# First block of a two-block kernel: modulation vector in PSUM, projections by blocks, another order of stages

## The chip, the core and the metric

The kernel runs on one core of a Trainium2 chip. A core has TensorE (PE, matrix products into PSUM), VectorE (DVE), ScalarE (ACT), GpSimd (POOL), and SyncE (SP), whose queue issues all the DMAs here. Each engine takes its own instructions in order and waits on semaphores. Times are microseconds on the device; less is better. PSUM has eight banks of 512 float32 per partition; GpSimd cannot reach them.

## What is computed

Two transformer blocks over 256 tokens of width 1024. Only the first part of the first block matters here, from its inputs to its gated outputs:

```python
sh1x, sc1x, g1x, sh2x, sc2x, g2x = jnp.split((jax.nn.silu(c) @ w_ada[l] + b_ada[l])[:, None, :], N_MOD, axis=-1)
sh1c, sc1c, g1c, sh2c, sc2c, g2c = jnp.split(jax.nn.silu(c_ctx) @ w_ada[l] + b_ada[l], N_MOD, axis=-1)
hc = _modulate(_rms_norm(ctx, norm1_g[l]), sh1c, sc1c)
s_f, s_b = _context_states(hc, w_in[l], gla_w2[l], gla_b2[l], s0)
hx = _modulate(_rms_norm(x, norm1_g[l]), sh1x, sc1x)
# _token_mixer(hx, ...):
z = h @ w_in
u, vs, q, r, ga, gb, k, v, lr = _split(z, IN_SPLITS)
a = _spatial_gating(gelu(u), gelu(vs), sgu_ln_g, sgu_ln_b, sgu_w, sgu_b)
o, s_f, s_b = _gla_bidir(qh, k, v, lr, gla_w2, gla_b2, s0f, s0b)
```

`_gla_bidir` is gated linear attention in both directions: the decays come from `log_sigmoid(lr @ w2 + b2)`, their running sums give exponentials by which queries and keys are scaled, and the state of the context enters the one of the tokens. All products are made as three matmuls of float32 values split into a rounded part and a remainder (`_hi` and `_lo`).

## The kernel before

**Weights.** All large weights pass through four slots (`w_raw`, `w_hi`, `w_lo`), a unit of 1024 x 128 at a time, 512 KB. SP loads a unit into `w_raw` once `lo_ready` says that GpSimd has made the remainder of the unit that stood there; ScalarE rounds it to `w_hi` when TensorE is done with the slot (`unit_used`), and GpSimd makes `w_lo` (L567) and raises `lo_ready`. The order is w_k (units 0 to 3), w_q (4 to 7), w_v (8 to 15), w_vs (16 to 23), w_u (24 to 31), w_r and so on.

**Modulation.** The first 16 vectors of the six modulations (shift and scale before the mixer) are made on TensorE: four products of `c2` with `adab` (L882), each two rows of 512, copied to `modrow`, transposed (L889) and added to biases on VectorE. The other 32 are made on VectorE, in 16 steps of `modulations(p0, p1)`: each multiplies two rows of `w_ada` (`adaw`, 1 MB, a ring of buffers filled by `ada_rows` on SP) with `csil`, the vector silu(c) in every partition, and sums along (L2364). `row_used` counts steps.

**Split inputs.** For each pair of eight k, VectorE makes the modulated input into `hfull`, ScalarE the same rounded into `a_hi` (`modulated(j)`), and VectorE the remainder `a_lo` (L2289, `split_ready`).

**Order on TensorE.** The four products with `c2`, with the means of squares between them; `w_k` (L640, 512 columns: tokens and context), tile after tile; the low-rank projection `wlr` (L903); `w_q`; the eight logits (L914), which need VectorE's `lrs` remainder (`lr_ready`) and four banks; `w_v` by token (`lin_tokens`, L716, two units at a time, 256 columns); `scores(0)` (L933, L935), transposes of `ks` (`keys`, L949), `w_vs` in four pairs with `keys` and `states(0)` (L960, L964) between them, `scores(1)`, `keys(1)`, `w_u` with `states(1)` after its fourth tile, half of `w_r`, `spatial()` (L996), the rest of `w_r`, `outputs()`.

**VectorE and ScalarE between them.** `decays(d)` and `differences(d)` make running sums and their differences, ScalarE's `powers` and `key_powers` exponentials, `operands(d)` the scaled queries and keys for `scores(d)`. `layer_norm_stats` reads `vs`.

## Time and profile before

| | us |
|---|---|
| median of 3 runs | 1358.4 (1358.06 to 1359.99) |
| profiled execution | 1354.67 |
| its span, first to last instruction | 1352.8 |
| TensorE busy | 1306.9 (97%) |
| GpSimd busy | 880.7 (65%) |
| VectorE busy | 742.7 (55%) |
| ScalarE busy | 703.9 (52%) |
| mean granted TensorE clock | 0.982 of full |

The page of the profile gives busy shares, 40 slices of the span with the granted clock, and groups of instructions. Matmuls are pipelined, so the time of one is read from start to start and not from its duration. An "idle before" of TensorE is a wait; its releaser is inferred. The timeline merges neighbours of one kind.

### The profile page before, as it was taken

How to read it: one execution, taken by the hardware profiler on the slowest of the kernel's cores; microseconds unless marked ns; L12 is line 12 of the kernel's file. 1: busy time of each engine (PE TensorE's matmuls, PEld its weight loads, DVE VectorE, ACT ScalarE, POOL GpSimd, SP SyncE). 2: the span in 40 equal slices, each digit the busy share in tenths (PEclk: the TensorE clock that was granted, in tenths of full speed). 3: DMA queues.
4: the chain of work that ended last, by engine and by line, in shares of the span. 5: the costliest groups of instructions: out<-in, count | busy, mean ns of one | idle time of the engine just before them, and what ended most of it. 6: DMA issues, size and time to landing. Idle time of an engine off the chain costs nothing.

```text
span 1352.8 us, 28587 instructions
## 1 busy us (share of the span) xinstructions
PE 1306.9 (97%) x10351; PEld 1246.8 (92%) x10351; DVE 742.7 (55%) x1539; ACT 703.9 (52%) x1232; POOL 880.7 (65%) x367
## 2 busy tenths in 40 slices
PE   8889989999999999999999999999999999999996
PEld 3579889999989999998889999999999999999996
DVE  4899994221465565256636326655552676555632
ACT  2555435354455555458333225756665555666653
POOL 0453667478859887956223223888888787888794
PEclk9989989999999999999899899999999999999999
DMA  8864345345536555744212112555555554555562
GB/s 327 340 244 171 133 149 199 114 139 183 176 125 203 183 176 167 193 138 145 65 62 66 60 54 88 172 179 178 172 172 185 174 185 151 189 177 183 164 183 74
DMA packets 60837, 217.75 MB, mean 161 GB/s; under 512 B 9832, under 2 KB 11112, under 8 KB 57936
## 3 DMA queue, kind: packets, MB, share of 16 engines
q1 hardware_dynamic: 60752, 216.56, 49.2%
q8 instruction: 61, 1.00, 0.3%
q14 instruction: 24, 0.20, 0.0%
HBM read 215.48 MB, written 1.05 MB: 160 GB/s over the span
## 4 chain that ended last, share of the span: by engine, by line
issue 44%; POOL 38%; PE 15%; ACT 1%; POOLq 1%; DVE 1%; ACTq 0%; DVEq 0%
POOL w_lo L567 38%; PE bank L663 9%; PE bank L742 5%; POOLq L564 0%; ACT h L1422 0%; POOLq L566 0%; ACT w_hi L1422 0%; PE bank L601 0%; PE bank L786 0%; PE bank L602 0%; PE bank L606 0%; ACT bank L1422 0%; DVE bank L3120 0%; DVE bank L3205 0%; DVE a_lo L3167 0%
## 5 line engine op out<-in xcount | busy, mean ns | idle before, releaser
L567 POOL TENSOR_TENSOR w_lo<-w_raw,w_hi 128x1024 fp32r<-128x1024 f32 x356 | 876.6, 2475 | 455.0 <-ACT w_hi L1422 454.6
L1422 ACT ACTIVATE w_hi<-w_raw 128x1024 fp32r<-128x1024 f32 x356 | 375.1, 1057 | 145.1 <-PE bank L742 49.8
L663 PE MATMUL bank<-a_hi,w_hi 128*128 128x256 f32 (+4 forms) x1032 | 293.4, 284 | 1.1 <-POOL w_lo L567 1.0
L663 PE MATMUL bank<-a_hi,w_lo 128*128 128x256 f32 (+4 forms) x1032 | 293.0, 284 | 0.0
L663 PE MATMUL bank<-a_lo,w_hi 128*128 128x256 f32 (+4 forms) x1032 | 292.8, 284 | 0.0
L640 PE MATMUL bank<-a_hi,w_hi 128*128 128x256 f32 (+3 forms) x752 | 224.2, 298 | 4.0 <-DVE a_lo L2289 3.1
L640 PE MATMUL bank<-a_lo,w_hi 128*128 128x256 f32 (+3 forms) x752 | 220.3, 293 | 0.0
L640 PE MATMUL bank<-a_hi,w_lo 128*128 128x256 f32 (+3 forms) x752 | 220.3, 293 | 0.0
L663 PEld LDWEIGHTS bank<-a_hi,w_hi 128*128 128x128 f32 x1032 | 195.8, 190 | 1.5 <-POOL w_lo L567 1.2
L663 PEld LDWEIGHTS bank<-a_lo,w_hi 128*128 128x128 f32 x1032 | 195.8, 190 | 0.1
L663 PEld LDWEIGHTS bank<-a_hi,w_lo 128*128 128x128 f32 x1032 | 195.9, 190 | 0.0
L640 PEld LDWEIGHTS bank<-a_hi,w_hi 128*128 128x128 f32 x752 | 146.8, 195 | 8.7 <-DVE a_lo L2289 4.5
L640 PEld LDWEIGHTS bank<-a_lo,w_hi 128*128 128x128 f32 x752 | 146.7, 195 | 1.2
L640 PEld LDWEIGHTS bank<-a_hi,w_lo 128*128 128x128 f32 x752 | 146.2, 194 | 1.4
L3241 DVE SCALAR_TENSOR_TENSOR bank<-row_mean,cols,bank 128x260 f32<-128x260 f32 (+3 forms) x112 | 54.7, 488 | 123.0 <-ACT cols L1422 117.7
L742 PE MATMUL bank<-g_hi,w_hi 128*128 128x256 f32 x352 | 99.2, 282 | 1.6 <-DVEq L2653 1.1
L742 PE MATMUL bank<-g_hi,w_lo 128*128 128x256 f32 x352 | 99.3, 282 | 0.0
L742 PE MATMUL bank<-g_lo,w_hi 128*128 128x256 f32 x352 | 98.8, 281 | 0.0
L2612 DVE SCALAR_TENSOR_TENSOR cbuf<-bank,pv,cbuf 128x189 f32<-128x189 f32 (+2 forms) x176 | 65.9, 425 | 48.5 <-ACT cbuf L1422 48.1
L742 PEld LDWEIGHTS bank<-g_hi,w_hi 128*128 128x128 f32 x352 | 66.4, 189 | 2.1 <-issue 1.2
L742 PEld LDWEIGHTS bank<-g_lo,w_hi 128*128 128x128 f32 x352 | 66.2, 188 | 0.0
L742 PEld LDWEIGHTS bank<-g_hi,w_lo 128*128 128x128 f32 x352 | 66.2, 188 | 0.0
(447 smaller groups left out, 2582.3 us busy)
## 6 DMA issues: line engine op xcount, KB each, us to landing
w_raw<-in_s SPq DMA_DIRECT2D x284, 512.0 KB, 3.6
w_raw<-in_down SPq DMA_DIRECT2D x48, 512.0 KB, 3.6
adaw<-in_w_ada SPq DMA_DIRECT2D x16, 1024.0 KB, 7.4
w_raw<-in_down SPq DMA_DIRECT2D x24, 384.0 KB, 3.2
adab<-in_w_ada_first SPq DMA_DIRECT2D x4, 2048.0 KB, 9.4
ctxt<-in_ctx SPq DMA_DIRECT2D x1, 1024.0 KB, 11.9
x<-in_x SPq DMA_DIRECT2D x1, 1024.0 KB, 18.6
out_h<-h SPq DMA_DIRECT2D x4, 256.0 KB, 2.7
```

Of the source, the lines that this page charges most:

```text
L567: pool.tensor_tensor(w_lo[:, s], w_raw[:, s], w_hi[:, s].bitcast(F32), ALU.subtract) \
L640: ins = mm(banks[s][:, first:n], w_[:, s, k], x_[:, k, first:n], start=(m == 0), stop=(m == 3 * KD - 1))
L663: ins = mm(banks[bank][:, tk], w_[:, s, k], x_[:, k, tk], start=(m == 0), stop=(m == 3 * KD - 1))
L742: ins = mm(banks[j][:, first:n], w_[:, s, k], x_[:, k0 + k, first:n], start=(m == 0), stop=(m == 3 * KF - 1))
L1422: return nc.scalar.activation(out_, in_, f, **kw)
L2612: v.scalar_tensor_tensor(dst, frm(banks[banks_of(p)[0]][:, 0:n]), pv[:, ds(pair + w, 1)], dst, ALU.mult, ALU.add).then_inc(conv_seq, 1)
L3241: return v.scalar_tensor_tensor(dst, row_mean[:, N2 - dst.shape[-1]:], by, dst, ALU.mult, ALU.add)
```

## The change

- `csil` is made by ScalarE into banks 4 and 5, and a step of `modulations` becomes four products of 512 columns instead of two of 1024; the sums of the halves go to `mod[:, 0]` and `mod[:, 1]` and are added later. The ring has seven buffers, and SP issues `ada_rows` at other places.
- `adab` is loaded and waited for in halves; averages, `pv` and `ctxt` follow the first. The warm-up matmuls use zeros of `part_sum`. The modulated input goes to banks 4 and 5 instead of `hfull`, and the gain is made from the product of bias and norm weight made before.
- `w_k` runs k 0 to 5 of all four tiles, then k 6 and 7.
- `w_q` comes before `wlr`; the logits stand one by one between matmuls of `w_v` and use two banks.
- `w_v` and `w_vs` run by blocks of k over all four slots, 512 columns. From the second group of `w_v` to the first four units of `w_u`, ScalarE and GpSimd round by blocks too, and `lo_ready` rises by four at a group's end.
- Both groups of `w_vs` come before `scores(0)`; `keys`, `states(0)`, `scores(1)` and `states(1)` stand between tiles of `w_u`.
- `operands(d)` is cut into `queries_keys` and `decayed_keys`; the steps of `modulations` all come before `decays(0)`.
- One ScalarE table set serves Abs, Exp and Ln.

```diff
-        ADA_RING = [0, 1, 2, 3, 0, 1, 2, 3, 0, 1, 4, 0, 1, 0, 1, 1]
+        ADA_RING = [5, 6, 0, 1, 2, 3, 4, 5, 6, 0, 1, 4, 0, 1, 4, 0]
...
+        GROUP0, GROUPS = UNIT0["w_v"] + SLOTS, 4
...
-                sp.dma_start(adab[j % 2][:], a["w_ada_first"][j]).then_inc(ada_in[j % 2], 16)
+                for half in range(2):
+                    ks_ = slice(4 * half, 4 * half + 4)
+                    sp.dma_start(adab[j % 2][:, ks_], a["w_ada_first"][j][:, ks_]).then_inc(ada_in[j % 2][half], 16)
                 if j == 0:
+                    small(averages[:], a["averages"], ctx_in)
+                    small(pv[:], a["pv"], ctx_in)
                     small(ctxt[:], a["ctx"], ctx_in)
...
+                    for p in range(7, 11):
+                        ada_rows(p)
                     slot_units(8, 9)
-                    ada_rows(4)
-                    ada_rows(5)
...
+                    ada_rows(11)
+                    slot_units(9, 13)
                     ada_rows(12)
...
+            remainders(0, GROUP0)
+            for g in range(GROUPS):
+                with pool.Fori(0, KD) as k:
+                    pool.wait_ge(block_hi, k + (8 * g + 1))
+                    pool.tensor_tensor(w_lo[:, :, ds(k, 1)], w_raw[:, :, ds(k, 1)], w_hi[:, :, ds(k, 1)].bitcast(F32), ALU.subtract) \
+                        .then_inc(block_lo, 1)
+                pool.wait_ge(block_lo, 8 * g + 8)
+                pool.sem_inc(lo_ready, SLOTS)
...
+            for s in range(4):
+                pe.wait_ge(lo_ready, s + 1)
+                pe.wait_ge(banks_free, s + 1)
+                if s >= 2:
+                    pe.wait_ge(mod_taken, s + 1)
+                tile_blocks(s, 0, 6)
+                if s == 0:
+                    flip_rows(3)
+            for s in range(4):
+                tile_blocks(s, 6, KD).then_inc(unit_used, 1)
...
+            def by_blocks(name, tiles, g, beside=None):
+                u0 = UNIT0[name] + SLOTS * g
+                own = [(t if tiles == 4 else 2 * g + t) for t in range(tiles)]
+                if u0 < GROUP0:
+                    pe.wait_ge(lo_ready, u0 + SLOTS)
+                for k in range(KD):
+                    if u0 >= GROUP0:
+                        pe.wait_ge(block_lo, 2 * (u0 - GROUP0) + k + 1)
+                    for t, b in enumerate(own):
...
+                        for i, (x_, w_) in enumerate(((a_hi, w_hi), (a_lo, w_hi), (a_hi, w_lo))):
+                            ins = mm(banks[b][:, :].rearrange("p (u m) -> p u m", u=SLOTS), x_[:, k, tk], w_[:, :, k],
+                                     start=(k == 0 and i == 0), stop=(k == KD - 1 and i == 2))
...
+            by_blocks("w_vs", 2, 0)
+            by_blocks("w_vs", 2, 1)
+            pe.wait_ge(small_in, 48)
             scores(0)
             keys(0, (0, 1))
-            lin_tokens("w_vs", 2, 0)
+            lin("w_u", N1, half0, tiles=(0, 1))
             keys(0, (2, 3))
-            lin_tokens("w_vs", 2, 1)
+            lin("w_u", N1, half0, tiles=(1, 3))
             states(0)
-            lin_tokens("w_vs", 2, 2)
-            lin_tokens("w_vs", 2, 3)
+            lin("w_u", N1, half0, tiles=(3, 5))
             scores(1)
             keys(1, (0, 1))
-            lin("w_u", N1, half0, tiles=(0, 2))
+            lin("w_u", N1, half0, tiles=(5, 6))
             keys(1, (2, 3))
-            lin("w_u", N1, half0, tiles=(2, 4))
+            lin("w_u", N1, half0, tiles=(6, 8))
             states(1)
-            lin("w_u", N1, half0, tiles=(4, 8))
...
-            fn(csil[:], csil[:], ACT.Silu).then_inc(csil_ready, 1)
+            for b in range(2):
+                fn(banks[4 + b][:, :], csil[:, b * 512:(b + 1) * 512], ACT.Silu).then_inc(csil_ready, 1)
...
                     for t in range(2):
-                        ins = v.scalar_tensor_tensor(adaw[ring][:, t], adaw[ring][:, t], 1.0, csil[:], ALU.mult,
-                                                     ALU.mult, accum_out=mod[:, 0, 16 + 2 * p + t:17 + 2 * p + t])
+                        for b in range(2):
+                            part = adaw[ring][:, t, b * 512:(b + 1) * 512]
+                            ins = v.scalar_tensor_tensor(part, part, 1.0, banks[4 + b][:, :], ALU.mult, ALU.mult,
+                                                         accum_out=mod[:, b, 16 + 2 * p + t:17 + 2 * p + t])
```

TensorE at the logits, before: they stand in a row between `w_q` (L640) and `w_v` (L716).

```order
L640 MATMUL bank<-a_lo,w_hi 128x256
L640 MATMUL bank<-a_hi,w_lo 128x256
L914 MATMUL bank<-lrs,w2s 128x512 [waits w2_split,lr_ready]
L914 MATMUL bank<-lrs,w2s 128x512 x3
L914 MATMUL bank<-lrs,w2s 128x512 [waits z_abs,t_ready] x4
```

The same place after, inside the second block of `w_v` (L957):

```order
L939 MATMUL bank<-lrs,w2s 128x512
L957 MATMUL bank<-w_hi,a_hi 128x512
L957 MATMUL bank<-w_hi,a_lo 128x512
L957 MATMUL bank<-w_lo,a_hi 128x512
L939 MATMUL bank<-lrs,w2s 128x512 [waits z_abs,t_ready]
L957 MATMUL bank<-w_hi,a_hi 128x512
```

The logits moved from between two projections into the first group of `w_v`. Next GpSimd, before: one loop over units for all the weights of the region.

```order
L567 TENSOR_TENSOR w_lo<-w_raw,w_hi 128x1024 [waits hi_ready]
L566 REGISTER_ALU
L567 TENSOR_TENSOR w_lo<-w_raw,w_hi 128x1024 [waits hi_ready]
L566 REGISTER_ALU
L567 TENSOR_TENSOR w_lo<-w_raw,w_hi 128x1024 [waits hi_ready]
```

After, one of four loops of eight that follow the first twelve units:

```order
L580 UNCONDITIONAL_BRANCH
L580 ISA
L582 ISA [waits block_hi]
L582 TENSOR_TENSOR w_lo<-w_raw,w_hi 128x4x128
L580 REGISTER_ALU
L580 COMPARE_AND_BRANCH
L580 UNCONDITIONAL_BRANCH [waits block_lo]
```

Sixteen units are done a block of four slots at a time, and the value that SP waits for is raised behind the last block. TensorE behind `w_vs`, after:

```order
L957 MATMUL bank<-w_lo,a_hi 128x512
L992 MATMUL bank<-qd_114,ki_117 128x128 [waits t_ready,kd_ready,z_abs,qk_ready,small_in]
L994 MATMUL bank<-qd_114,kd 64x64
...
L1010 MATMUL bank<-ident,ks 128x128 [waits row_used,ks_ready]
L1010 MATMUL bank<-ident,ks 128x128 x7
L656 MATMUL bank<-a_hi,w_hi 128x256 [waits banks_free,lo_ready]
```

Between the end of `w_vs` and the first tile of `w_u` (L656) only `scores(0)` and two `keys` are left.

## Rows read from the trace of the kernel before

**Rows 1.** Stretches: us, busy of each engine, granted clock, DMA share, GB/s.

```profile
core 0: us, PE busy (x) PEld busy (x) DVE busy (x) ACT busy (x) POOL busy (x), PEclk, DMA share, GB/s
40.00:60.00 20.00, 16.22 (x60) 10.21 (x59) 17.73 (x27) 12.94 (x20) 10.61 (x5) 0.91 0.83 312
80.00:100.00 20.00, 15.61 (x99) 13.95 (x98) 18.69 (x20) 12.42 (x18) 13.18 (x4) 0.79 0.49 171
100.00:120.00 20.00, 20.00 (x161) 20.00 (x161) 17.24 (x19) 12.06 (x9) 6.59 (x2) 0.95 0.38 141
180.00:200.00 20.00, 16.37 (x89) 13.62 (x88) 19.72 (x25) 7.76 (x9) 10.61 (x4) 0.74 0.35 108
```

**Rows 2.** TensorE in order of time, start to first projection; start, duration, idle before.

```profile
12.64 7.03 PE L882 MATMUL bank<-adab,c 128*2 128x512 f32 x16 [1.35 <-DMA adab<-in_w_ada_first]
43.30 0.40 PE L889 MATMUL bank<-ident,modrow 2*128 2x2 f32 x4
44.66 0.50 PE L640 MATMUL bank<-a_hi,w_hi 128*128 128x512 f32 x1
50.84 0.79 PE L640 MATMUL bank<-a_hi,w_hi 128*128 128x512 f32 x1 [3.13 <-DVE a_lo L2289]
```

**Rows 3.** TensorE in order of time, the stages' first instructions up to `spatial`'s end.

```profile
71.82 0.40 PE L903 MATMUL bank<-a_hi,wlr_hi 128*96 128x512 f32 x1
77.38 0.28 PE L640 MATMUL bank<-a_hi,w_hi 128*128 128x256 f32 x1
88.88 1.09 PE L914 MATMUL bank<-lrs,w2s 96*128 96x512 f32 x4
94.36 2.77 PE L914 MATMUL bank<-lrs,w2s 96*128 96x512 f32 x4 [4.39 <-DVE la L2382]
96.93 0.41 PE L716 MATMUL bank<-w_hi,a_hi 128*128 128x256 f32 x1
145.20 0.39 PE L933 MATMUL bank<-qd,ki 128*128 128x128 f32 x2
150.51 1.09 PE L949 MATMUL bank<-ident,ks 128*128 128x128 f32 x8
165.73 3.72 PE L960 MATMUL bank<-vc,spare_hi 128*128 128x256 f32 x16 [1.76 <-ACT spare_hi L1422]
170.83 0.47 PE L716 MATMUL bank<-w_hi,a_hi 128*128 128x256 f32 x1
186.46 0.46 PE L933 MATMUL bank<-qd,ki 128*128 128x128 f32 x2 [3.63 <-issue]
214.42 0.47 PE L640 MATMUL bank<-a_hi,w_hi 128*128 128x256 f32 x1
237.63 0.61 PE L996 MATMUL bank<-sguw,vs 128*128 128x128 f32 x4
241.12 0.36 PE L640 MATMUL bank<-a_hi,w_hi 128*128 128x256 f32 x1
```

**Rows 4.** VectorE in order of time: products with `csil`, `vs`, adds with PSUM.

```profile
56.98 1.22 DVE L2364 SCALAR_TENSOR_TENSOR adaw<-adaw,csil 128x1024 f32<-128x1024 f32 x1 [0.47 <-ACT csil L1422]
...
59.28 3.41 DVE L2364 SCALAR_TENSOR_TENSOR adaw<-adaw,csil 128x1024 f32<-128x1024 f32 x1
...
226.25 3.31 DVE L2500 TENSOR_TENSOR vs<-vs,rows 128x1024 f32<-128x1024 f32 x1
240.16 2.50 DVE L2511 TENSOR_TENSOR bank<-bank,rows 128x512 f32<-128x512 f32 x4 [10.61 <-PE bank L996]
```

**Rows 5.** GpSimd's timeline and groups; DMA issues with KB and us to landing.

```profile
138.48 7.67 POOL L567 TENSOR_TENSOR w_lo<-w_raw,w_hi 128x1024 fp32r<-128x1024 f32 x2 [6.53 <-ACT w_hi L1422]
...
L567 POOL TENSOR_TENSOR w_lo<-w_raw,w_hi 128x1024 fp32r<-128x1024 f32 x356 | 876.6, 2475 | 455.0 <-ACT w_hi L1422 454.6
L578 POOL TENSOR_TENSOR h<-h,part_sum 128x256 f32<-128x256 f32 x4 | 2.8, 725 | 9.5 <-ACT part_sum L1422 9.5
...
adab<-in_w_ada_first SPq DMA_DIRECT2D x4, 2048.0 KB, 9.4
...
adaw<-in_w_ada SPq DMA_DIRECT2D x1, 1024.0 KB, 4.9
...
w_raw<-in_s SPq DMA_DIRECT2D x4, 512.0 KB, 3.4
```

More of the change, by code:

```diff
@@ L500, in slot_units @@
                             stream_unit(name, u, u % SLOTS)
-                    slot_units(4, 8)
                     sp.wait_ge(std_ready, 2)
                     sp.wait_ge(ada_done, 3)
-                    for p in range(4):
-                        ada_rows(p)
+                    ada_rows(0)
+                    ada_rows(1)
+                    slot_units(4, 5)
+                    ada_rows(2)
+                    ada_rows(3)
+                    slot_units(5, 6)
+                    ada_rows(4)
+                    slot_units(6, 7)
+                    ada_rows(5)
+                    sp.wait_ge(ada_done, 4)
+                    ada_rows(6)
+                    slot_units(7, 8)
                     sp.wait_ge(w2_clear, 1)
@@ L699, in up @@
                 pairs(pe, 4, KF, pair_of_tiles)
-            def lin_tokens(name, tiles, pair=None):
-                u0, t0 = UNIT0[name], TILE0[name]
-                def two(it, s):
-                    pe.wait_ge(lo_ready, it * 4 + (u0 + s + 2))
-                    pe.wait_ge(banks_free, it * 4 + (t0 + s + 2))
-                    for t in range(tiles):
-                        dst = banks[s + t * 2 // tiles][:, 256 * (t % (tiles // 2)):][:, 0:256] \
-                            .rearrange("p (u m) -> p u m", u=2)
-                        tk = slice(t * P, t * P + P)
-                        n = 0
-                        for k in range(KD):
-                            wh, wl = w_hi[:, s:s + 2, k], w_lo[:, s:s + 2, k]
-                            for x_, w_ in ((a_hi, wh), (a_lo, wh), (a_hi, wl)):
-                                ins = mm(dst, x_[:, k, tk], w_, start=(n == 0), stop=(n == 3 * KD - 1))
-                                n += 1
-                    ins.then_inc(unit_used, 2)
-                if pair is not None:
-                    two(pair // 2, 2 * (pair % 2))
-                    return
-                with pe.Fori(0, TILES_OF[name] // 4) as it:
-                    for s in (0, 2):
-                        two(it, s)
             def down(i, n, its=(0, 2), first=0):
@@ L896, in _, with mod_rows @@
-            lin("w_k", 2 * N1, whole, S_X, tiles=(0, 4))
+            def mod_rows(j, beside=None):
+                if j >= 2:
+                    pe.wait_ge(modrow_ready, j - 1)
+                for k in range(KD):
+                    if k % 4 == 0:
+                        pe.wait_ge(ada_in[j % 2][k // 4], 16 * (j // 2) + 16)
+                    ins = mm(banks[6 + j % 2][0:2, :], c2[:, k], adab[j % 2][:, k], start=(k == 0), stop=(k == KD - 1))
+                    if k == 3 and beside is not None:
+                        beside()
+                ins.then_inc(ada_done, 1)
@@ new lines, in flip_rows, with mean_square @@
+            def flip_rows(j):
+                pe.wait_ge(modrow_ready, j + 1)
+                if j >= 2:
+                    pe.wait_ge(mod_taken, j - 1)
+                for i in range(4):
+                    ins = nc.tensor.transpose(banks[2 + j % 2][:, 2 * i:2 * i + 2],
+                                              modrow[:, j % 2, i * P:(i + 1) * P], ident[0:2, 0:2])
+                ins.then_inc(mod_flipped, 1)
+            def mean_square(i):
+                pe.wait_ge(ctx_in, 48)
+                pe.wait_ge(sum_ready, i + 1)
+                mm(banks[4 + i][:, 0:N1], over_d, (sq, sqx)[i][:, 0, 0:N1], start=True, stop=True).then_inc(ms_ready, 1)
@@ new lines, in tile_blocks @@
+            def tile_blocks(s, k0, k1_):
+                for k in range(k0, k1_):
+                    if s == 0:
+                        pe.wait_ge(split_ready, 8 * S_X + k + 1)
+                    for i, (w_, x_) in enumerate(((w_hi, a_hi), (w_hi, a_lo), (w_lo, a_hi))):
+                        ins = mm(banks[s][:, :], w_[:, s, k], x_[:, k], start=(k == 0 and i == 0), stop=(k == KD - 1 and i == 2))
+                return ins
+            mod_rows(0)
+            mod_rows(1, lambda: mean_square(RMS_CTX))
@@ L898, in _ @@
+            lin("w_q", N1, half0, tiles=(0, 4))
             pe.wait_ge(wlr_rest, 1)
@@ L905, in _, with logits @@
             ins.then_inc(lr_done, 1)
-            lin("w_q", N1, half0, tiles=(0, 4))
-            pe.wait_ge(lr_ready, 1)
-            pe.wait_ge(w2_split, 1)
-            for i in range(2 * HG):
+            def logits(i):
                 d, hh = divmod(i, HG)
-                if i >= 4:
-                    pe.wait_ge(t_ready, i - 3)
-                    pe.wait_ge(z_abs, i - 3)
-                mm(banks[4 + i % 4][:, :], w2s[:, d, hh * DK:(hh + 1) * DK], lrs[:], start=True, stop=True) \
+                if i >= 2:
+                    pe.wait_ge(t_ready, i - 1)
+                    pe.wait_ge(z_abs, i - 1)
+                mm(banks[6 + i % 2][:, :], w2s[:, d, hh * DK:(hh + 1) * DK], lrs[:], start=True, stop=True) \
@@ L919, in scores, with logits_beside @@
+            def logits_beside(k, t):
+                if k == 0 and t == 0:
+                    pe.wait_ge(lr_ready, 1)
+                    pe.wait_ge(w2_split, 1)
+                n = 4 * (k - 1) + t
+                if 0 <= n < 2 * HG:
+                    logits(n)
+            by_blocks("w_v", 4, 0, logits_beside)
+            by_blocks("w_v", 4, 1)
             def scores(d):
```

285 lines of the change are left out of this document (150 added, 135 removed).

## The prediction

> **What bounds the kernel now.** I read the page first: TensorE is busy 97% of the span, so a stage is worth what TensorE loses in it. The stretches of 20 us come next [rows 1]: in the first 260 us, where the change lies, the granted clock is 0.91, 0.79, 0.95 and 0.74 in four of them, which at levels of 1.2 and 2.4 GHz is 3.6, 8.4, 2.0 and 10.4 us at the lower one. TensorE's own rows in order of time [rows 2, 3] tell what stood before each fall: a wait of 3.13 us for `a_lo` inside the first projection, one of 4.39 us for `la` between the logits, one of 3.63 us ahead of the second scores. The reader is to see there that between these points matmul follows matmul: 96 of 256 columns take 77.38 to 88.88, 0.120 us each, and 24 of 512 take 71.82 to 77.38, 0.232 us each. So this region is a chain of TensorE's work plus waits, and what comes behind it (from 241.12) is not touched and only shifts. The sum below is therefore a new timetable of TensorE up to 241.12, the end of `spatial`.
>
> **Vectors' rows.** VectorE is nearly full from 57 to 200 us [rows 1]. Its products with `csil` take 1.22 us, and 3.41 us when GpSimd works beside them [rows 4]; eleven of the 32 are of the long kind, 24 us in all. The change puts `csil` into PSUM, and every product is then of 512 columns with one operand there. The nearest row is a 512-column add with a PSUM operand, four in 2.50 us [rows 4], 0.60 us from start to start: four per step of `modulations`, 2.45 us a step with the accumulator read, against 2.3 alone and up to 6.8 beside GpSimd. The Trainium skill, "SBUF — State Buffer", section "Who interferes with whom", says that a VectorE instruction with at most one SBUF input, outside the two-port modes, does not contend with GpSimd. By that rule the 24 us go away entirely, and I take it so, since 0.60 us is also what the PSUM rows show.
>
> **Start, up to the first projection.** Before: the first rows of weights land at 12.64, the four products with `c2` take 7 us each, and the fourth ends at 43.30 [rows 2]. Now `adab` comes in halves, and averages, `pv` and `ctxt` queue behind the first; 1.1 MB instead of 2.7 MB stand ahead of the first matmul. 2 MB take about 9.4 us to land [rows 5], so I put the first half at 8.0, the second product at 17.3 (its data, 4.8 MB deep in the queue), and the rest back to back: 17.3 + 3 x 7.0 + 1.9 for means and transposes = 40.2. That is 3.1 us earlier; bounds 0 (the last transfers set the end as now) and 4.6 (12.64 - 8.0, no wait for the second).
>
> **First projection.** Before 43.30 to 71.82, 28.5 us, of which 96 x 0.23 = 22 are matmuls, 3.1 the wait and 1.7 the lower clock [rows 1, 2]. Now the four tiles run k 0 to 5 first, so the last two splits have 12 us of matmuls as cover. The short wait at k=4 stays (ScalarE's order is unchanged, `modulated(2)` ends near 47), about 2 us. I get the first matmul at 41.9, flip of the fourth row at 48.6, 54 matmuls to 60.8, 24 to 66.3: 5.5 us earlier than 71.82. The Trainium skill, "VectorE: DVE Perf Modes", section "Why PSUM operands drop a tier", has fp32 `tensor_scalar` at half rate once an operand is in PSUM; as an estimate from it the 16 of them would cost 0.1 us more each, some 0.8 us of it on the path, and the sum would be 66.3 or 67.1.
>
> **Low-rank projection and logits.** `w_q` and `wlr` change places, 17.1 us together as before: 83.4 against 88.88. The eight logits took 88.88 to 96.93, 8.05 us for 1.9 of work [rows 3]; now each stands beside three matmuls of `w_v`, 0.92 us apart, in which ScalarE's Abs (0.6) and VectorE's add (0.67) fit. Two waits are put in their place. SP stands at `ada_rows(11)` until seven steps of `modulations` are done (55.2 + 7 x 2.45 = 72.4, the 55.2 as below), and units 9 to 11 of `w_v` queue behind it: the four slots are ready at 84.8, 1.4 us late. And TensorE waits for `lr_ready`, behind eleven steps on VectorE, which I let begin at 55.2, 1.8 earlier than the 56.98 of [rows 4]: 55.2 + 27 + 1.2 + 2.3 + 0.7 = 86.4 at most, 1.1 us. Bounds: 0 and 4 (steps of 2.7 us).
>
> **w_v.** 384 matmuls of 256 become 192 of 512, 192 x 0.2265 = 43.5 us. 84.8 + 43.5 + 1.9 + 1.1 = 131.2 against 145.20. So 14.0 us are won up to here.
>
> **From there to the end of `spatial`.** Before 145.20 to 241.12, 95.9 us [rows 3]. The work in it: `w_vs` 192 x 0.12 = 23.2, two scores of 5.3 (145.20 to 150.51), four transposes of 0.8, two states of 5.1 (165.73 to 170.83), 192 matmuls of `w_u` and 96 of `w_r` at 0.121 (214.42 to 237.63 is 192) = 34.7, `spatial` 3.5: 85.4. The other 10.5 us are waits of 1.8 and 3.6 and the lower clock. `w_vs` with 512 columns is 21.7, so the work falls to 83.9. What the new order adds is the point of this prediction. By blocks, `lo_ready` of a group rises only when GpSimd has done all eight blocks of it, and the four transfers of the next group wait for that. **Refill one:** the units of `w_vs`'s second half are issued 2.4 us after `w_v` ends. One unit lands after 3.4 us, 1 MB after 4.9 [rows 5], so 1.5 us per 512 KB more: four in about 7.8. With rounding 0.6 and one block on GpSimd 1.3 that is 12.1, and `w_vs`'s first half lasts 10.9: wait 1.2. **GpSimd's pace:** 2.4 us for 1024 columns, 0.72 for 256 [rows 5], so 1.27 for 512; TensorE takes a block in 1.36. But `queries_keys(1)` runs just then with three two-input operations of 1.2 us in SBUF; such pairs take turns, as two GpSimd operations in 7.67 us instead of 4.8 show [rows 5]. Wait 3.2 (0 to 4). **Refill two:** `w_u`'s first four units can be issued only when `w_vs`'s last block is done, 1.4 us before TensorE ends with it. Then 7.8 + 0.6 + 8 x 1.27 + 1.3 for `differences(1)` in its way = 19.9, from there 18.5 after the end of `w_vs`. TensorE has scores and two transposes, 6.2 us, to fill that, since all other work stands behind `w_u`'s first tile. Wait 12.3. Bounds: 9 (landing 6, blocks 1.15) and 16 (blocks of 1.5, two operations in the way). Such an idle time is followed by the lower clock, as each of the three of over 3 us was: 2.5 us, bounds 1.7 and 5. **spatial** had 23.2 us between `states(1)` and its start, now 11.6, and VectorE's normalisation of `vs` took 15.1 (214.42 to 229.56 [rows 4]): 1.6 us for its second half. Sum: 83.9 + 1.2 + 3.2 + 12.3 + 2.5 + 1.6 = 104.7, and 131.2 + 104.7 = 235.9 against 241.1: **5.2 us less**. For the loop around each GpSimd block, a wait and an address from a register that no row shows, I take 0.05 us x 16 = 0.8: **4.4 us less**.
>
> **Where the changes put it.** The three places in the order: the logits lie between matmuls of `w_v` on TensorE; SP issues the groups in fours behind one value; GpSimd has loops of eight around one block.
>
> **Rivals.** (A) The refill is mostly hidden: blocks on GpSimd near 1.0 us, landing in 6, no lower clock. Wait 8.5 instead of 12.3, no 2.5, no contention in `w_vs`: 4.4 + 3.8 + 2.5 + 3.2 = 13.9 us less, 1344.5. For it: the 7.8 us of landing is extrapolated. Against it: `lo_ready` cannot come before the eighth block. If the start brings the whole 4.6 too, 1343. (B) Slower: **GpSimd sets the pace of sixteen exposed blocks**, eight in `w_vs` and eight ahead of `w_u`. Each 0.1 us more per block costs 1.6 us; from 1.27 + 0.05 on, 1.6 us per block gives +4.5, even with the time before, and 1.9, with two-input operations of VectorE in turn with most of them, gives 9.3 - 4.4 = +4.9, 1363. For it: the turns above, and the dynamic address. It decides from 1.6 us per block. (C) No change to be seen: the start brings nothing (its last transfers set 43.30, -3.1) and the four slots or `lr_ready` come 2 us later: 4.4 - 3.1 - 2 = 0.7 more, 1359. (D) The products with PSUM are no quicker beside GpSimd (against the rule above): eight GpSimd operations of 2.2 us stand in eleven steps, `lr_ready` comes 14 us late: +10, 1368. The PSUM rows at 0.60 us speak against it.
>
> **The numbers.** The profiled execution is 1354.67 us with a span of 1352.8, the median of the three runs 1358.4. 4.4 off the first is 1350.3; off the median, 1354.0, which I predict, since that is what will be compared. Chances: forecast 0.50 (its own range 1349 to 1358), A 0.20, B 0.13, C 0.13, D 0.04. The range that holds eight in ten leaves out the lower half of A and most of B and D: 1342 to 1362. A measurement can tell 0.2% (2.7 us) from no change. Faster by more: three quarters of the forecast and A, 0.57; within: the rest of it and C, 0.26; slower, B and D: 0.17.
>
> **What would show it.** In the changed kernel: the first product at 8 and the fourth ending near 40; no wait over 2.5 us in the first projection; `w_v` ending near 131, all its matmuls 0.2265 us apart; VectorE's 512-column products at 0.6 us with no long ones; the first unit of `w_u` about 12 us after the transposes of `ks`, released by GpSimd's `w_lo`, with the clock low around it; sixteen GpSimd blocks of 1.3 us. Wrong would be a forecast with no such wait (then A or better), or a wait of TensorE over 3 us anywhere earlier.

## The result and the profile after

| | us |
|---|---|
| changed kernel, median of 5 runs | 1365.41 (1363.89 to 1368.74) |
| kernel before, median of 5 runs beside it | 1358.22 (1358.06 to 1359.99) |
| ratio | 1.0055, 95% interval 1.0038 to 1.0072 |
| profiled execution and its span | 1364.66, 1362.9 |

The change makes the kernel slower by half a per cent; the forecast was 1354.0, 0.3% faster. The same stretches as in [rows 1], now of the changed kernel, and one more, 140 to 160, in which TensorE was busy all the 20 us before:

```profile
40.00:60.00 20.00, 17.62 (x77) 13.78 (x78) 16.85 (x44) 10.73 (x18) 7.71 (x4) 1.00 1.01 418
80.00:100.00 20.00, 15.69 (x56) 11.07 (x55) 7.03 (x15) 9.04 (x14) 7.01 (x3) 0.83 0.57 215
100.00:120.00 20.00, 20.00 (x89) 16.56 (x89) 19.21 (x46) 14.69 (x17) 10.69 (x7) 1.00 0.28 106
140.00:160.00 20.00, 9.38 (x37) 7.07 (x37) 17.95 (x21) 4.43 (x7) 9.80 (x8) 0.83 0.29 105
180.00:200.00 20.00, 11.16 (x74) 11.17 (x75) 9.91 (x18) 10.97 (x16) 11.15 (x7) 0.66 0.30 106
```

The first stretch is better than before, the last two have TensorE busy for half of their time. TensorE's rows at the stage boundaries, answering to [rows 2] and [rows 3], say where:

```profile
7.50 7.03 PE L873 MATMUL bank<-adab,c 128*2 128x512 f32 x16
...
38.97 0.40 PE L884 MATMUL bank<-ident,modrow 2*128 2x2 f32 x4
40.73 0.50 PE L901 MATMUL bank<-a_hi,w_hi 128*128 128x512 f32 x1 [1.35 <-POOL w_lo L575]
...
65.61 0.39 PE L656 MATMUL bank<-a_hi,w_hi 128*128 128x256 f32 x1
...
87.22 0.79 PE L957 MATMUL bank<-w_hi,a_hi 128*128 128x512 f32 x1 [4.31 <-POOL w_lo L575]
...
135.90 0.47 PE L957 MATMUL bank<-w_hi,a_hi 128*128 128x512 f32 x1
...
158.39 0.79 PE L957 MATMUL bank<-w_hi,a_hi 128*128 128x512 f32 x1 [10.06 <-POOL w_lo L582]
...
171.83 0.38 PE L992 MATMUL bank<-qd,ki 128*128 128x128 f32 x2
...
188.84 0.58 PE L656 MATMUL bank<-a_hi,w_hi 128*128 128x256 f32 x1 [10.61 <-POOLq L585]
...
247.61 2.05 PE L1057 MATMUL bank<-sguw,vs 128*128 128x128 f32 x16 [1.48 <-DVE vs L2607]
249.41 0.37 PE L656 MATMUL bank<-a_hi,w_hi 128*128 128x256 f32 x1
```

`w_k` ends at 65.61 (before 71.82) and `w_v` at 135.90 (145.20), so 9.3 us are still won there. Then come 10.06 us of idle time between the halves of `w_vs` and 10.61 ahead of `w_u`; `spatial` ends at 249.41 against 241.12, 8.3 us late. The span is 10.1 longer, so 1.8 us lie behind, where nothing was looked at.

What TensorE waited for is GpSimd's `w_lo` both times (L585 raises `lo_ready` behind a group's last block). GpSimd's groups of eight blocks (L582), ScalarE's roundings that start them, and SP's issues:

```profile
109.31 13.94 POOL L582 TENSOR_TENSOR w_lo<-w_raw,w_hi  x8 [22.14 <-ACT w_hi L1483]
132.36 13.81 POOL L582 TENSOR_TENSOR w_lo<-w_raw,w_hi  x8 [9.10 <-ACT w_hi L1483]
156.37 10.68 POOL L582 TENSOR_TENSOR w_lo<-w_raw,w_hi  x8 [10.20 <-ACT w_hi L1483]
176.83 11.90 POOL L582 TENSOR_TENSOR w_lo<-w_raw,w_hi  x8 [9.78 <-ACT w_hi L1483]
...
101.19 7.39 ACT L1483 ACTIVATE ebuf<-ebuf 128x4096 f32<-128x4096 f32 x3
108.48 3.74 ACT L1483 ACTIVATE w_hi<-w_raw 128x512 fp32r<-128x512 f32 x7
131.52 3.76 ACT L1483 ACTIVATE w_hi<-w_raw 128x512 fp32r<-128x512 f32 x7 [1.79 <-DMA w_raw<-in_s]
155.54 2.19 ACT L1483 ACTIVATE w_hi<-w_raw 128x512 fp32r<-128x512 f32 x4 [15.76 <-DMA w_raw<-in_s]
...
123.33 1.75 SPq L441 DMA_DIRECT2D w_raw<-in_s  x4
146.39 44.77 SPq L441 DMA_DIRECT2D w_raw<-in_s  x12
```

Read them as one chain. GpSimd's first group starts at 109.31, right behind ScalarE's Exp and Ln (101.19 to 108.58), and ends at 123.25; SP issues four units at 123.33; ScalarE gets them at 131.52; GpSimd's second group runs 132.36 to 146.17; SP issues at 146.39; ScalarE gets them at 155.54. From the start of one group to the start of the next that is 23.1, 24.0 and 20.5 us, with GpSimd, the queue or ScalarE's rounding at work nearly all the time and TensorE's 10.9 us of `w_vs` per group beside it. The profile's chain of waits for this stretch goes through these three (start, us, what):

```profile
118.93 4.34 POOL w_lo L582 x2
...
124.65 6.69 DMA w_raw<-in_s
131.52 3.77 ACT w_hi L1483 x7
...
138.93 7.25 POOL w_lo L582 x5
...
148.64 6.72 DMA w_raw<-in_s
```

### The profile page after: what moved, and what is told of

Its sections match the earlier page's. It is cut to its first block, busy times and chain, and to the rows that moved or that the text cites. A ratio compares the mean times of both kernels' runs of the same rounds, so it can differ in the third digit from the quotient of the medians.

```text
span 1362.9 us, 28180 instructions
## 1 busy us (share of the span) xinstructions
PE 1304.3 (96%) x10063; PEld 1231.3 (90%) x10063; DVE 708.5 (52%) x1606; ACT 700.9 (51%) x1242; POOL 870.8 (64%) x383
## 4 chain that ended last, share of the span: by engine, by line
issue 41%; POOL 37%; PE 16%; ACT 3%; DMA 1%; POOLq 1%; DVE 1%; SPq 0%; ACTq 0%; DVEq 0%
POOL w_lo L575 35%; PE bank L679 9%; PE bank L732 5%; POOL w_lo L582 2%; DMA w_raw<-in_s 1%; ACT w_hi L1483 1%; PE bank L957 1%; ACT ebuf L1483 0%; POOLq L572 0%; ACT h L1483 0%; POOLq L574 0%; SPq L441 0%; PE bank L617 0%; PE bank L776 0%; PE bank L618 0%
## 5 line engine op out<-in xcount | busy, mean ns | idle before, releaser
L575 POOL TENSOR_TENSOR w_lo<-w_raw,w_hi 128x1024 fp32r<-128x1024 f32 x340 | 816.6, 2414 | 423.6 <-ACT w_hi L1483 423.2
L1483 ACT ACTIVATE w_hi<-w_raw 128x1024 fp32r<-128x1024 f32 (+1 forms) x372 | 375.8, 1019 | 169.2 <-PE bank L732 50.5
L656 PE MATMUL bank<-a_hi,w_hi 128*128 128x256 f32 (+2 forms) x720 | 212.6, 295 | 11.5 <-POOLq L585 10.6
L656 PE MATMUL bank<-a_hi,w_lo 128*128 128x256 f32 (+2 forms) x720 | 209.1, 290 | 0.0
L656 PE MATMUL bank<-a_lo,w_hi 128*128 128x256 f32 (+2 forms) x720 | 209.0, 290 | 0.0
L679 PEld LDWEIGHTS bank<-a_hi,w_hi 128*128 128x128 f32 x1032 | 196.1, 190 | 1.5 <-POOL w_lo L575 1.2
L679 PEld LDWEIGHTS bank<-a_lo,w_hi 128*128 128x128 f32 x1032 | 196.2, 190 | 0.1
L679 PEld LDWEIGHTS bank<-a_hi,w_lo 128*128 128x128 f32 x1032 | 196.2, 190 | 0.0
L656 PEld LDWEIGHTS bank<-a_hi,w_hi 128*128 128x128 f32 x720 | 141.8, 197 | 14.2 <-POOLq L585 10.8
L656 PEld LDWEIGHTS bank<-a_lo,w_hi 128*128 128x128 f32 x720 | 141.8, 197 | 0.1
L656 PEld LDWEIGHTS bank<-a_hi,w_lo 128*128 128x128 f32 x720 | 141.6, 197 | 0.0
L582 POOL TENSOR_TENSOR w_lo<-w_raw,w_hi x32 | 50.3, 1610 | 51.2 <-ACT w_hi L1483 51.2
L732 PEld LDWEIGHTS bank<-g_lo,w_hi 128*128 128x128 f32 x352 | 66.3, 188 | 0.0
```

The lines of the kernel that those rows point to most:

```text
L575: pool.tensor_tensor(w_lo[:, s], w_raw[:, s], w_hi[:, s].bitcast(F32), ALU.subtract) \
L582: pool.tensor_tensor(w_lo[:, :, ds(k, 1)], w_raw[:, :, ds(k, 1)], w_hi[:, :, ds(k, 1)].bitcast(F32), ALU.subtract) \
L656: ins = mm(banks[s][:, first:n], w_[:, s, k], x_[:, k, first:n], start=(m == 0), stop=(m == 3 * KD - 1))
L679: ins = mm(banks[bank][:, tk], w_[:, s, k], x_[:, k, tk], start=(m == 0), stop=(m == 3 * KD - 1))
L732: ins = mm(banks[j][:, first:n], w_[:, s, k], x_[:, k0 + k, first:n], start=(m == 0), stop=(m == 3 * KF - 1))
L1483: return nc.scalar.activation(out_, in_, f, **kw)
```

## The experiments

The theory at this point: (T) the cycle of a group, that is eight blocks on GpSimd, four transfers behind the eighth, rounding and blocks again, is 20 to 24 us long, starts late, and TensorE has 10.9 us of `w_vs` per group to spend. Rivals: (R1) the order of TensorE's stages; (R2) GpSimd's pace beside VectorE, wherever the chain starts; (R3) the PSUM vector brings less than thought. A yardstick for all runs: where the first matmul behind `spatial` starts, since the median less that start is 1114 to 1118 us for every kernel but one, which is named. Gains and losses are differences of medians from the changed kernel's 1365.41; the kernel before, run beside each experiment, had 1357.0 to 1357.6 against 1358.2 beside the changed kernel, so about 1 us of each means nothing.

### by_units: the blocks undone

`GROUPS` is 0, `w_v` and `w_vs` run as before (two units, 256 columns), ScalarE and GpSimd go by units everywhere. Start, PSUM vector and order of stages stay; the places of `w_v`'s roundings and copies among ScalarE's powers change with the blocks.

```diff
-        GROUP0, GROUPS = UNIT0["w_v"] + SLOTS, 4
+        GROUP0, GROUPS = UNIT0["w_v"] + SLOTS, 0
...
-            by_blocks("w_v", 4, 0, logits_beside)
-            by_blocks("w_v", 4, 1)
+            lin_tokens("w_v", 4, 0, logits_beside)
+            for p_ in range(1, 4):
+                lin_tokens("w_v", 4, p_)
...
-            by_blocks("w_vs", 2, 0)
-            by_blocks("w_vs", 2, 1)
+            for p_ in range(4):
+                lin_tokens("w_vs", 2, p_)
```

> The changed kernel with the blocks undone in w_v and w_vs: TensorE runs two units at a time with 256 columns, ScalarE and GpSimd round a unit at a time everywhere, lo_ready rises by one; the stage order, PSUM vector and start stay. Theory (the cycle of a group: four slots come back only 20 to 23 us after their predecessors' first block, 10.7 to 13.9 us of GpSimd blocks, 8.2 to 9.1 us of landing and 0.9 of rounding, against 10.9 us of w_vs per group): the waits of 10.06 us inside w_vs and 10.61 us ahead of w_u go, down to 1 to 3 us in all, while w_v and w_vs get 4 us longer by their columns; w_vs ends near 160 instead of 171.8 and spatial near 235 instead of 249.4, so 1348 to 1354. Rival (the order of stages is what costs: nothing but scores and keys between w_vs and w_u, whatever the rounding): the wait ahead of w_u stays above 6 us and the time above 1358. Rival (VectorE's contention with GpSimd): GpSimd's units take over 3 us each beside VectorE and w_vs waits as long as before, 1362 or more.

Measured: 1346.58 us, ratio to before 0.9912 (0.9889 to 0.9935); the stage behind `spatial` starts at 230.42. TensorE's waits from 80 to 200 us (total, times, longest):

```profile
PE bank L956 <- POOL w_lo L575: 7.5, 4, 4.9
PE bank L956 <- DVE lrs L2475: 0.7, 1, 0.7
```

The wait ahead of `w_u` is gone although the order of stages is unchanged, so R1 falls as the cause of the two waits. The blocks, with the order of ScalarE that belongs to them, cost 18.8 us, and without them the rest of the change is a gain of 0.9%. GpSimd is no quicker here: four units beside VectorE take

```profile
139.07 15.35 POOL L575 TENSOR_TENSOR w_lo<-w_raw,w_hi 128x1024 fp32r<-128x1024 f32 x4 [6.53 <-ACT w_hi L1479]
```

where a group of blocks took 13.8. So its slow pace alone does not make waits of 10 us; together with the release of four slots at once it does.

### half_refills: the same blocks, but transfers beside them

SP loads the units of three groups in halves of four k, the first halves as soon as four of the eight blocks are done. ScalarE waits for the half that it rounds.

```diff
-                    slot_units(16, 20)
+                    for g in range(1, GROUPS):
+                        for half in range(2):
+                            sp.wait_ge(block_lo, 8 * g - 4 + 4 * half)
+                            ks_ = slice(4 * half, 4 * half + 4)
+                            for s in range(SLOTS):
+                                u = GROUP0 + SLOTS * g + s
+                                sp.dma_start(w_raw[:, s, ks_], a[name][u][:, ks_]) \
+                                    .then_inc(landed[s] if half else half_in, 16)
```

> The changed kernel, but the units of three groups (w_vs and the first half of w_u) are loaded in halves of four k: SP issues the four first halves as soon as four of GpSimd's eight blocks are done, and the four others behind the eighth. Theory (the serial cycle blocks, landing, blocks): the landing lies beside GpSimd's blocks for half of its time. A half lands in 5 to 6 us; the first block of w_vs's second group is ready near 147 instead of 157.8, and the wait of 10.06 falls to 0 to 2; the wait ahead of w_u falls from 10.61 to 3 to 6. Time 12 to 18 us less: 1347 to 1353. Rival (the transfers are bound by their bytes, halves land no sooner): the waits stay within 3 us of what they are, 1360 to 1365.

Measured: 1350.86 us, 0.9946 (0.9927 to 0.9965), behind `spatial` at 235.59. Its waits, and GpSimd's last three groups:

```profile
PE bank L965 <- POOL w_lo L590: 5.5, 6, 1.6
PE bank L965 <- POOL w_lo L583: 5.0, 1, 5.0
PE bank L664 <- POOLq L593: 3.1, 1, 3.1
```

```profile
131.84 15.36 POOL L590 TENSOR_TENSOR w_lo<-w_raw,w_hi  x8 [7.19 <-ACT w_hi L1491]
147.62 16.95 POOL L590 TENSOR_TENSOR w_lo<-w_raw,w_hi  x8 [0.42 <-ACT w_hi L1491]
164.99 10.79 POOL L590 TENSOR_TENSOR w_lo<-w_raw,w_hi  x8 [0.42 <-ACT w_hi L1491]
```

GpSimd's idle time between the last three groups falls from 10 to 0.4 us, and 14.6 us of the time go. It is the serial landing, not the blocks as such. What is left in `w_vs` is six short waits at GpSimd's pace: the two groups beside VectorE take 1.9 and 2.1 us a block, the last, alone, 1.35. The 5.0 is the wait ahead of `w_v`, and 3.1 stay ahead of `w_u`.

### w_u_by_unit: only the last group by units

`GROUPS` is 3, and ScalarE rounds `w_u`'s first four units one by one.

> The changed kernel, with only the last of the four groups, w_u's first four units, rounded a unit at a time. Theory (ahead of w_u the wait is the landing plus eight blocks, of which w_u's first tile needs only one unit): the wait falls by 8 blocks less one unit, 11.9 less 2.5 us, less one rounding more: from 10.61 to 1 to 4 us; the wait of 10.06 in w_vs stays. Time 7 to 10 us less, with the lower clock behind the wait gone too: 1355 to 1358. Rival (the landing of the four units sets it): the wait falls by under 3 us, 1362 to 1365.

Measured: 1357.7 us, 0.9994 (0.998 to 1.0008). The wait of 10.61 is now (us in total, times, longest)

```profile
PE bank L656 <- POOL w_lo L575: 4.4, 1, 4.4
```

and the one inside `w_vs` is still 9.5. Refill two was the landing plus eight blocks; 6.2 of the 10.6 us went when `w_u` no longer waited for all eight, and 4.4 us stay, a little more than the 4 at most that I had expected.

### group0_early and reset_psum: where the chain starts, and its pace

group0_early moves ScalarE's first roundings ahead of and between Exp and Ln, and those of the next group between the powers:

```diff
+            blocks(0, 0, 3)
             act.wait_ge(z_abs, 8)
             link(fn(ebuf[:], ebuf[:], ACT.Exp, scale=-1.0))
+            blocks(0, 3, 5)
```

> The changed kernel, only ScalarE's order altered: the first block roundings of w_v's second group stand among Exp and Ln instead of behind them (they started at 108.5), and those of w_vs's first group among the powers instead of behind them (131.5). Theory (the chain starts late because ScalarE's 7.4 us of Exp and Ln stand ahead of it): GpSimd's first eight blocks start near 102 instead of 109.3, end near 117 instead of 123.3, each later group lands 6 to 8 us earlier, the wait inside w_vs falls from 10.06 to 2 to 5 us; the wait ahead of w_u stays at 9 to 12, since it hangs on w_vs's own end. Time 7 to 10 us less: 1355 to 1359. Rival (GpSimd's pace of 1.73 us a block beside VectorE sets the chain, wherever it starts): the blocks get slower by as much as they start earlier, and the wait inside w_vs stays above 8 us, 1363 or more.

Measured: 1362.7 us, 1.0042 (1.0026 to 1.0059): 2.7 us gained, where I expected 7 to 10, and the interval overlaps the changed kernel's (1.0038 to 1.0072), so the time alone shows no gain. The first group starts at 102.11 as it should, and a block takes 1.28 us while VectorE is at its products with PSUM. The second starts 6.4 us earlier, but

```profile
125.92 17.80 POOL L582 TENSOR_TENSOR w_lo<-w_raw,w_hi  x8 [9.03 <-ACT w_hi L1483]
...
128.21 8.71 DVE L2508 TENSOR_TENSOR_SCAN ebuf<-reset,la 128x512 f32<-128x512 f32 x4
```

now has all four scans of `decays(1)` beside it, takes 2.2 us a block, and ends only 2.5 us earlier. The wait in `w_vs` is 8.0 and the one ahead of `w_u` 11.5. So R2 is nearly right: the chain does start earlier, but the pace gives most of it back.

reset_psum keeps the changed kernel and moves one operand of the eight scans, the mask of ones and zeros, from SBUF to a PSUM bank:

```diff
-                    ins = v.tensor_tensor_scan(dst, reset[:], src, 0.0, ALU.mult, ALU.add)
+                    ins = v.tensor_tensor_scan(dst, banks[4][:, :], src, 0.0, ALU.mult, ALU.add)
```

> The changed kernel, but the mask of ones and zeros that the eight scans of decays multiply by stands in a PSUM bank instead of SBUF; nothing else is altered. Theory (GpSimd's blocks of 1.73 us beside VectorE, 1.33 alone, are the turns that it takes with VectorE's two-SBUF-operand instructions, the scans among them): the scans take 1.1 to 1.2 us each instead of 1.4 to 1.9, GpSimd's blocks beside them 1.3; the first group ends 2 to 3 us earlier and the second 2, so the wait of 10.06 falls to 5 to 8 and the time by 2 to 6 us: 1359 to 1363. Rival (a scan's time and GpSimd's are set by something else, such as its own bandwidth): the same durations, 1364 to 1366.

Measured: 1361.74 us, 1.0027 (1.0015 to 1.0038), in the range expected. GpSimd's first two groups, then VectorE's scans:

```profile
110.00 12.12 POOL L582 TENSOR_TENSOR w_lo<-w_raw,w_hi  x8 [22.52 <-ACT w_hi L1483]
130.75 12.05 POOL L582 TENSOR_TENSOR w_lo<-w_raw,w_hi  x8 [8.64 <-ACT w_hi L1483]
...
119.75 4.57 DVE L2503 TENSOR_TENSOR_SCAN ebuf<-bank,la 128x512 f32<-128x512 f32 x4
128.88 4.57 DVE L2503 TENSOR_TENSOR_SCAN ebuf<-bank,la 128x512 f32<-128x512 f32 x4
```

Four scans take 4.57 us, where four took 7.64 and 5.63 in the changed kernel, and a group of blocks 12.1 instead of 13.9 (13.0 to 15.0 in the profiles of late_rows, w_u_by_unit and scores_between, which keep the mask in SBUF; the blocks average 1.5 us, not the 1.3 expected). The wait in `w_vs` is 7.8. It is not PSUM that is quick: in group0_early four scans with the mask in SBUF ran while GpSimd stood idle, and took the same:

```profile
119.08 4.57 DVE L2508 TENSOR_TENSOR_SCAN ebuf<-reset,la 128x512 f32<-128x512 f32 x4
```

The Trainium skill, "SBUF — State Buffer", section "Who interferes with whom", says that a VectorE instruction with two SBUF inputs contends with a GpSimd instruction that reads SBUF; the trace agrees for the scan.

### scores_between: other work into the gap

```diff
             by_blocks("w_vs", 2, 0)
-            by_blocks("w_vs", 2, 1)
             pe.wait_ge(small_in, 48)
             scores(0)
+            by_blocks("w_vs", 2, 1)
```

> The changed kernel with one stage of TensorE moved: scores(0), 5.3 us, between the two groups of w_vs instead of behind them. Theory (TensorE stands idle from 148.3 to 158.4 while the group is loaded and rounded, whatever it could do instead): scores(0) starts at 151.8, when kd is ready, and ends near 157, so it costs nothing there and w_vs still ends near 170 to 172; the wait ahead of w_u grows by the same 5.3 us, since the transfers of w_u's units hang on w_vs's last block: 10.6 becomes 15 to 16, and the time stays at 1363 to 1367; only the lower clock may come less often. Rival (TensorE's order is what costs): 5 us less, 1360.

Measured: 1368.3 us, 1.0082 (1.0065 to 1.0099). The wait ahead of `w_u`:

```profile
PE bank L656 <- POOLq L585: 16.0, 1, 16.0
```

3.3 us are left in `w_vs`, 16.0 stand ahead of `w_u`, and the stage behind `spatial` starts at 248.84, where it did. Filling this gap of the chain only moved it. (The median is 4.5 us above this run's profiled execution; why is open, so no loss is read from it.)

### late_rows: w_v's four slots

SP issues the rows of `w_ada` for steps 9 and 10 behind units 8 and 9, and those for step 11 behind unit 12.

```diff
-                    for p in range(7, 11):
-                        ada_rows(p)
+                    ada_rows(7)
+                    ada_rows(8)
                     slot_units(8, 9)
-                    ada_rows(11)
-                    slot_units(9, 13)
+                    ada_rows(9)
+                    slot_units(9, 10)
+                    ada_rows(10)
+                    slot_units(10, 13)
+                    ada_rows(11)
```

> The changed kernel, only SP's order altered: the rows of w_ada for steps 9 and 10 are issued behind units 8 and 9, and those for step 11 behind unit 12. Theory (w_v's first four slots are late because four megabytes of rows stand ahead of unit 8 in the queue: it was issued at 65.6 and landed at 75.2): unit 8 lands near 71, GpSimd goes through units 8 to 11 without a stop and is done near 82.5 instead of 87.2; the wait of 4.31 us ahead of w_v falls under 1, and the lower clock behind it (6.9 us in the changed kernel) goes; w_v ends near 127 instead of 134.9, but the wait inside w_vs grows by 2 to 6, since GpSimd's second group still comes behind Exp and Ln, which come earlier by 4 to 5 only if the logits do. Time 3 to 7 us less: 1358 to 1362. Rival (GpSimd's own time for four units, 9.4 us, sets it): the wait stays above 3, no difference.

Measured: 1361.63 us, 1.0033 (1.002 to 1.0046). The wait is 2.3 instead of 4.3 us, not under 1: unit 8 now follows unit 7 on GpSimd without a stop, but units 10 and 11 are still late. The direction and the time fit, the mechanism only in part. Even the 2.0 us are not all the edit's: in this profile `w_k` ends at 67.14 instead of 65.61 (the granted clock of 44 to 54 us is 0.83 instead of 1.00), so TensorE came to `w_v` later, and `w_v` starts at 86.75, only 0.5 us earlier. The profiles of w_u_by_unit and scores_between, without this edit, have the same late `w_k`, waits of 3.2 and 3.1 us and `w_v` at 87.5; against them the edit is worth 0.8 us. Where the rest of the 3.8 us of the median comes from is open, and its interval reaches the changed kernel's.

### csil_sbuf and units_csil: what the PSUM vector is worth

The vector stays in SBUF, in the changed kernel and in by_units; the products keep 512 columns (and SP waits for the last step before `sguw`, which takes the vector's place).

```diff
-                            ins = v.scalar_tensor_tensor(part, part, 1.0, banks[4 + b][:, :], ALU.mult, ALU.mult,
+                            ins = v.scalar_tensor_tensor(part, part, 1.0, csil[:, b * 512:(b + 1) * 512], ALU.mult, ALU.mult,
```

> The changed kernel with one operand moved: silu(c) stays in SBUF instead of two PSUM banks; the products are still of 512 columns. Theory (the PSUM operand is what keeps VectorE's products clear of GpSimd): beside GpSimd's units the products take 2 to 3 us instead of 0.68 and GpSimd's units 3 us and more instead of 2.4; VectorE's eleven steps end 4 to 8 us later, the logits and with them w_v's start and ScalarE's Exp and Ln shift, and the wait inside w_vs with them: 1368 to 1376. Rival (the quicker steps bring nothing, since TensorE waits for GpSimd's units there anyway): within 2 us of 1365.

> by_units with silu(c) in SBUF instead of PSUM: what the PSUM vector is worth where no refill stands on the path. Theory (VectorE's steps end some 10 us later, and the logits, ScalarE's Exp and Ln and VectorE's decays with them; TensorE waits for w_v's slots and for the logits' operand): 8 to 18 us more than by_units, 1355 to 1365, so that the rest of the change without the blocks brings about nothing by itself. Rival (the loss of csil_sbuf was mostly the refill chain shifted): under 5 us more than by_units.

Measured: 1383.5 us, 1.0192 (1.0175 to 1.0209), and 1368.56 us, 1.0079 (1.0055 to 1.0104). Both lose more than expected: 18 us against the changed kernel and 22 us against by_units. The 64 products, in SBUF (csil_sbuf) and then in PSUM (the changed kernel), total and mean ns:

```profile
L2476 DVE SCALAR_TENSOR_TENSOR adaw<-adaw,csil 128x512 f32<-128x512 f32 x64 | 65.7, 1095 | 0.4 <-ACT csil L1484 0.3
```

```profile
L2475 DVE SCALAR_TENSOR_TENSOR adaw<-adaw,bank 128x512 f32<-128x512 f32 x64 | 39.3, 684 | 0.3 <-ACT bank L1483 0.3
```

R3 falls: PSUM takes 26 us off VectorE, and 18 to 22 us arrive in the time. A large part arrives through SP's queue: units 9 to 11 of `w_v` stand behind the rows of step 11, which wait for VectorE's seventh step. SP issued these rows at 82.23 in csil_sbuf, at 70.76 in the changed kernel, and the wait ahead of `w_v` is 14.0 us instead of 4.3. What the vector would be worth with another order on SP was not tried. units_csil is slower than the kernel before, so without PSUM the rest of the change is no gain, with or without blocks. What the order of TensorE's stages is worth alone was not tried.

### units_all, blocks_all and units_mid: both ways to mend it

units_all is by_units with late_rows, reset_psum, and ScalarE's `powers(1)` behind the rounding of `w_v`'s last units. blocks_all keeps the blocks and joins group0_early, half_refills, w_u_by_unit, late_rows and reset_psum. units_mid is units_all with `scores(0)` between the second and third pair of `w_vs`.

> The changed kernel with three edits together: w_v and w_vs by units (by_units), the scans' mask in PSUM (reset_psum), SP's later rows (late_rows), and ScalarE's powers(1) behind the rounding of w_v's last two units, so that these don't wait for VectorE's scans. Theory (with units no refill stands on the path, and what is left is GpSimd's turns with VectorE and the rounding held up by powers(1)): of the 4.85 us that TensorE waits inside w_vs 3 to 4 go, of the 2.08 us inside w_v 1; 1341 to 1345 against 1346.6 for by_units. Rival (that wait is bound by something else, the transfers or the banks): 1346 to 1348.

> The changed kernel with its blocks kept, and the edits group0_early, half_refills, w_u_by_unit, late_rows and reset_psum together. Theory (the cycle of a group of four slots against 10.9 us of w_vs): the first group's blocks start near 101, halves land beside the blocks, and GpSimd's 8 x 1.3 us plus 0.4 is all that is left of the cycle, equal to TensorE's 10.9; both waits are under 3 us. 1341 to 1346. Rival (blocks are bound to lose, since eight blocks of four slots on GpSimd take 10.4 us against 9.4 by units and beside VectorE 14): 1347 to 1351.

> As units_all, with scores(0) between the second and the third pair of w_vs. Theory (with units an idle TensorE inside w_vs is filled by other work without delaying a refill, since slots come free pair by pair): what wait is left inside w_vs is filled, and the half-rate clock behind it goes: 0 to 3 us less than units_all. Rival (scores(0) is not ready by then: kd comes from VectorE near 149): TensorE waits for VectorE instead, 0 to 3 us more.

Measured: units_all 1339.71 us, 0.9863 (0.9843 to 0.9884); blocks_all 1340.22, 0.9867 (0.9844 to 0.989); units_mid 1344.4, 0.9903 (0.9884 to 0.9922). The waits of the first two from 80 to 200 us:

```profile
PE bank L959 <- POOL w_lo L578: 4.6, 3, 2.3
PE bank L959 <- DVE lrs L2476: 0.7, 1, 0.7
```

```profile
PE bank L667 <- POOL w_lo L586: 4.4, 1, 4.4
PE bank L968 <- POOL w_lo L586: 1.8, 1, 1.8
```

Both times are a little better than expected, though 4.4 us ahead of `w_u` stay in blocks_all, where under 3 were expected, and both have the stage behind `spatial` at 225.1. With the chain broken the two packages are worth the same. They differ in more than the blocks, so what blocks as such win or lose is not shown. In units_mid the wait inside `w_vs` stayed at 2.2 us (it lies ahead of the scores), and a new one of 3.4 us for the keys' copies came ahead of their transposes; neither account of it was right.

## Why the prediction was wrong

Step by step, by its own sum (us on TensorE's timetable):

| step | predicted | measured |
|---|---|---|
| fourth product with `c2` ends | 40.2 | 38.97 |
| `w_k` ends | 66.3 | 65.61 |
| `w_q` and `wlr` end | 83.4 | 82.9 |
| four slots of `w_v` | 84.8 | 87.2 |
| wait for the logits' operand | 1.1 | 0 |
| `w_v` ends | 131.2 | 135.9 |
| refill one and GpSimd's pace in `w_vs` | 1.2 + 3.2 | 10.06 + 1.5 |
| refill two | 12.3 | 10.61 |
| lower clock behind the two waits | 2.5 | 4.9 |
| `spatial`'s second half | 1.6 | 1.48 |
| `spatial` ends | 236.7 | 249.41 |

The sum held 0.8 us for the loop around GpSimd's blocks, 0.05 us each, for which no row stood. No run shows the loop by itself; three blocks in a row, loop included, took 3.82 us in group0_early, 1.27 each.

**Right:** the start, the first projection (no wait over 2.5 us), the products at 0.6 us with no long ones, `w_q` and `wlr`, the 0.1 us more for each of the 16 `tensor_scalar` into PSUM (0.54 us, where those in SBUF took 0.41), and the mechanism of refill two, which w_u_by_unit and half_refills confirm. Its size came near in part by luck: the units were issued 4.5 us before TensorE ended `w_vs`, not 1.4, and from issue to TensorE took 21.5 us, not 19.9.

**Wrong, the step that decided: refill one.** The prediction wrote that "the units of `w_vs`'s second half are issued 2.4 us after `w_v` ends". They were issued at 146.39, 10.5 us after. The step took the group before as paced by TensorE. But that group's blocks (132.36 to 146.17) hung on its own landing, and that on the blocks of the first group (109.31 to 123.25), which stood behind Exp and Ln. Walked from 109.31 with the prediction's own prices (eight blocks 10.2, landing and rounding 8.4, eight blocks 10.2) the issue comes at 138.0, 2.1 us after `w_v`: the chain had no slack, which the prediction did not see, but at these prices it would have lost nothing. What lost the 8.1 us were the two groups of blocks, 13.9 and 13.8 us long (7.4), and 0.7 of landing, and without slack they arrived in full. The wait grew from 1.2 to 10.06 by these 8.1 and by 2.3 between issue and first matmul (12.0 instead of 9.7), less 1.5 that TensorE itself took longer for the first half of `w_vs` (12.4 instead of 10.9). Its own sign of being wrong, a wait of over 3 us earlier than the one ahead of `w_u`, came twice: 4.31 and 10.06. With the pace inside `w_vs` (1.5 instead of 3.2) the step missed 7.2 of the 12.7 us. by_units and half_refills, which break the cycle in two ways, take 18.8 and 14.6 us off, with GpSimd as slow beside VectorE as before.

**Wrong in size: GpSimd's blocks.** 1.27 us predicted with turns beside `queries_keys(1)` only; measured 1.74 and 1.73 beside scans and two-operand instructions, 1.33 alone. The trace of before showed it: [rows 5] has two units in 7.67 us. I had priced it as one wait of 3.2 us in `w_vs`, but it acts one and two groups earlier, on when transfers start. reset_psum lowers this term: the wait in `w_vs` falls by 2.2 us and the median by 3.7. Rival B had the engine right but not the place: it wanted 1.6 us a block in the sixteen exposed blocks, and these took 1.33 and 1.49; the slow ones were the two groups that it left out.

**Wrong in size: `w_v`'s slots.** The wait was 4.31 us, not 1.4. Behind it matmuls stand 0.43 us apart instead of 0.23 up to 91.65, at a granted clock of 0.66 in 85 to 95 us, which cost 2.3 us more; the sum had nothing for it, nor for the 1 us that lies mostly between the logits' matmuls. The prediction looked at units 9 to 11, behind step seven (72.4 predicted, 70.76 measured), but unit 8 was late already: four megabytes of rows stand ahead of it in the queue, and issued at 65.58 it reached ScalarE at 75.23. late_rows shows the direction, with 0.5 to 1 us on `w_v`'s start.

**Rivals.** B's 1363, D's 1368 and C's 1359 all came nearer than my forecast, but by luck, since none did so by its own steps: no exposed block took 1.6 us, and the start did bring its gain (C's other half, four slots 2 us later, came true). D fell: the products were quick, and csil_sbuf shows that without them the changed kernel is 18 us slower.

## What to carry over

When several buffers are released together, write the refill as a cycle (work on the old contents, issue, landing, work on the new) and walk it from the first group to the last before comparing it with what the consumer does per group: where the chain has no slack, what one group loses is passed on to every group after it. Here loading in two halves, or releasing buffers one by one, broke the cycle, and putting work into the gap only moved it. And price a GpSimd instruction by what VectorE does beside it, for each group apart.
